# Two expert weight loads issued before the last four modulation blocks, and two gate diagonals built after the head norm, in a two-layer diffusion trunk

## What is computed

```python
for i in range(DEPTH):                       # DEPTH = 2
    sh1, sc1, g1, sh2, sc2, g2 = modulation(cvec, w_ada[i], b_ada[i])   # for c_ctx and for c
    h = rmsnorm(x, norm_g[i, 0]) * (1.0 + sc1) + sh1
    if i % 2 == 0:
        y, s = hgrn2_mixer(h, hgrn_w_in, lb, hgrn_onorm_g, hgrn_w_out, s0)
    else:
        y = diff_attn_out(diff_attention(q, k, v, lam), attn_subln_g, lam_init, attn_w_out)
    x = x + g1 * y
    h = rmsnorm(x, norm_g[i, 1]) * (1.0 + sc2) + sh2
    x = x + g2 * hier_moe(h, w_group, b_group, w_expert, b_expert, w_gate, w_up, w_down)
# the end of the HGRN2 mixer: a norm over each head, a SiLU gate, the output matrix
o = rmsnorm(o, onorm_g) * silu(g)
return o @ w_out
```

## Time and profile before

| | |
|---|---|
| time, median of 3 runs | 1291.94 us (1291.27 to 1293.31) |
| profiled execution: its own time | 1291.27 us |
| profiled execution: span | 1289.5 us |
| PE busy | 1127.8 us (87%) |
| DVE busy | 427.3 us (33%) |
| ACT busy | 228.2 us (18%) |
| POOL busy | 135.8 us (11%) |
| bytes moved | 316.78 MB, mean 246 GB/s |

### The profile page before, as it was taken

The page is one execution under the profiler, slowest core; times in us unless marked ns, Lnnn a source line. Parts: engine busy times, 40 slices in busy tenths (PEclk is TensorE's granted clock), DMA queues, the critical chain, the costliest instruction groups (busy, mean ns, idle before and its releaser), DMA issues.

```text
span 1289.5 us, 20237 instructions
## 1 busy us (share of the span) xinstructions
PE 1127.8 (87%) x8500; PEld 681.7 (53%) x8500; DVE 427.3 (33%) x1102; ACT 228.2 (18%) x527; POOL 135.8 (11%) x219
## 2 busy tenths in 40 slices
PE   4899999995999979998888499997779799988884
PEld 1566666664444465665665154443445656566651
DVE  1155555555512333000000754513853330000006
ACT  2201101110212222010001121104742221000110
POOL 0333333334000000000000300000000000000012
PEclk8899999997899979999999799998989799999997
DMA  9964444433557836999999952232001279999994
GB/s 342 290 203 131 132 132 132 132 132 132 180 201 267 352 142 263 409 428 427 426 426 426 396 211 89 78 118 98 1 1 52 80 277 419 427 426 427 426 425 169
DMA packets 97581, 316.78 MB, mean 246 GB/s; under 512 B 3792, under 2 KB 38912, under 8 KB 81120
## 3 DMA queue, kind: packets, MB, share of 16 engines
q1 hardware_dynamic: 90160, 298.05, 60.1%
q10 hardware_dynamic: 5248, 10.97, 2.2%
q0 software_dynamic: 2096, 6.67, 1.4%
HBM read 304.67 MB, written 11.01 MB: 245 GB/s over the span
## 4 chain that ended last, share of the span: by engine, by line
issue 71%; DVE 2%; DMA 2%; POOL 1%; PE 0%; POOLq 0%; DVEq 0%
DMA xn<-expert_rows,moe_row 2%; DVE xn L1520 1%; DVE moe_own L1518 0%; DVE xn L1523 0%; DVE moe_own L1530 0%; DVE hg_att L1563 0%; POOL x L1878 0%; POOL moe_own L1873 0%; DVE hg_tf L1580 0%; DVE hg_qaf L1600 0%; DVE hg_kf L1602 0%; DVE x L1535 0%; POOL hg_kb L1843 0%; POOL hg_qab L1841 0%; PE bank L702 0%
## 5 line engine op out<-in xcount | busy, mean ns | idle before, releaser
L566 PE MATMUL bank<-ring,moe_xe 128*64 128x256 f32 x2048 | 229.8, 380 | 29.5 <-DMA ring<-in_moe_w_up 16.9
L566 PEld LDWEIGHTS bank<-ring,moe_xe 128*64 128x64 f32 x2048 | 152.1, 137 | 111.3 <-DMA ring<-in_moe_w_up 21.4
L668 PE MATMUL bank<-uT,ring 128*128 128x384 f32 x384 | 137.3, 504 | 4.6 <-DMA ring<-in_hgrn_w_in 4.6
L581 PE MATMUL bank<-ring,moe_hT 128*64 128x512 f32 x512 | 118.3, 616 | 16.6 <-DMA ring<-in_moe_w_down 14.4
L855 PE MATMUL bank<-ring,uT 128*128 128x512 f32 x288 | 126.3, 593 | 1.3 <-issue 1.3
L1508 DVE TENSOR_TENSOR moe_hh<-moe_sg,bank 128x256 f32<-128x256 f32 x32 | 13.5, 422 | 324.1 <-ACT moe_sg L1032 324.1
L554 PE MATMUL bank<-moe_g,moe_h 128*128 128x128 f32 x768 | 96.7, 285 | 2.4 <-DVE moe_g L1405 2.4
L554 PEld LDWEIGHTS bank<-moe_g,moe_h 128*128 128x128 f32 x768 | 92.7, 200 | 7.9 <-issue 7.9
L668 PEld LDWEIGHTS bank<-uT,ring 128*128 128x128 f32 x384 | 70.8, 193 | 47.1 <-ACT uT L954 4.8
L1869 POOL TENSOR_TENSOR moe_flag<-con 128x1 f32<-128x1 f32 x2 | 0.4, 194 | 897.1 <-DMA expert_rows<-moe_oe 897.1
L855 PEld LDWEIGHTS bank<-ring,uT 128*128 128x128 f32 x288 | 53.6, 190 | 65.1 <-issue 65.1
(11 more groups left out here) (249 smaller groups left out, 1203.8 us busy)
## 6 DMA issues: line engine op xcount, KB each, us to landing
ring<-in_moe_w_gate SPq DMA_DIRECT2D x32, 2048.0 KB, 24.4
ring<-in_moe_w_up SPq DMA_DIRECT2D x32, 2048.0 KB, 26.3
ring<-in_moe_w_down SPq DMA_DIRECT2D x32, 2048.0 KB, 23.0
ring<-in_w_ada SPq DMA_DIRECT2D x24, 2048.0 KB, 10.3
ring<-in_hgrn_w_in SPq DMA_DIRECT2D x32, 512.0 KB, 6.6
ring<-in_attn_w_qkv SPq DMA_DIRECT2D x6, 2048.0 KB, 22.2
expert_rows<-moe_oe ACTq DMA_DIRECT2D x14, 512.0 KB, 10.3
ring<-in_hgrn_w_in SPq DMA_DIRECT2D x2, 2048.0 KB, 13.4
```

What stands on the lines that cost most here:

```text
L566: last = mm(bank[2 + e][64 * g:64 * g + 64, 256 * part:256 * part + 256], m["xe"][:, k, 64 * e:64 * e + 64], cols(slot)[:, k, 256 * g:256 ...
L581: last = mm(bank[5 + 2 * half][64 * e:64 * e + 64, :], m["hT"][:, e, j, 64 * g:64 * g + 64], down_rows(PART_SLOTS[n][4 + e])[:, g, j, 512 ...
L668: last = mm(to[:, 0:TOK], w[:, k, f, :], uT[:, k, :], start=(k == 0), stop=(k == KC - 1))
```

## The change

Two edits in one.

The first is in SP's part: the first two loads of expert weights of layer 0 (gate and up of expert 0, into slots 2 and 3) are issued behind block 7 of the next layer's modulation, no longer behind block 11. `experts(0)` leaves them out in its first pair.

The second is in VectorE's part: the diagonals for q = 0 and q = 1 are made behind the head norm, directly ahead of `gated(0)`.

```diff
@@ SP
                     for at, (slot, (name, e)) in enumerate(zip(PART_SLOTS[n], PARTS)):
-                        expert_weights(n, i, it, slot, name, e)
+                        if at >= 2 or n == 1 or not isinstance(it, int) or it > 0:
+                            expert_weights(n, i, it, slot, name, e)
...
-            for b in range(12):
+            for b in range(8):
+                ada(1, b % 2, b, 5 + b // 2)
+            for slot, (name, e) in zip(PART_SLOTS[0][0:2], PARTS[0:2]):
+                expert_weights(0, 0, 0, slot, name, e)
+            for b in range(8, 12):
                 ada(1, b % 2, b, 5 + b // 2)
             count = experts(0)
@@ VectorE
             dve.wait_ge(hg["o_out"], 8)
-            need(dve, 0, "mod_cols", 12)
-            gate_diagonal(0, HG["diag"], 2, 0, 0)
-            gate_diagonal(0, HG["diag"], 2, 0, 1)
             dve.wait_ge(late_in, LATE)
             head_norm(0, HG["s0"][:, 0:8, :].rearrange("p h d -> p (h d)"))
             head_norm_end(0, None)
...
+            need(dve, 0, "mod_cols", 12)
+            gate_diagonal(0, HG["diag"], 2, 0, 0)
+            gate_diagonal(0, HG["diag"], 2, 0, 1)
             gated(0)
             gate_diagonal(0, HG["diag"], 2, 0, 2)
             gated(1)
```

## The result

| | before | after |
|---|---|---|
| median of 4 runs | 1291.88 us (1291.27 to 1293.31) | 1307.84 us (1305.93 to 1312.56) |
| profiled execution: own time | 1291.27 us | 1305.98 us |
| profiled execution: span | 1289.5 us | 1304.1 us |

The changed kernel is slower: its time divided by that of before is 1.0128, 95% interval [1.0099, 1.0156]. I had said 1304.0 us, 1297.5 to 1307.0. The direction and each of the places were right; the median lies 3.8 us above the number and 0.8 us above the range.

What follows compares the result with a forecast made beforehand. The prediction took TensorE's own list to bound the stage of the change. Its terms, 4.7 + 2.4 + 4.2 + 2.3 - 0.5 = +13.1 us on 1291.27, gave 1304.4, stated as 1304 us, range 1297.5 to 1307.

Steps and rivals of the forecast that it cites:

- term 1: Ahead of the first gate product, TensorE waits for the first diagonal, now made behind the head norm: +4.7 us.
- term 2: Behind the wait for the first diagonal, TensorE's clock falls to 0.50: +2.4 us, bounds 0 and 2.6.
- term 3: In the modulation, block 8 lands late behind gate and up in SP's queue: +4.2 us, bounds 2.3 and 5.6.
- term 4: Behind the wait for block 8, TensorE's clock falls again: +2.3 us, bounds 0 and 2.6.
- term 5: Block 11 of the modulation, no longer queued beside gate and up, is not waited for: -0.5 us.
- head start: At the first expert matmul, gate and up landing some 32 us earlier wins nothing, as they were early already.
- What bounds the stage: From 333 to 440 us TensorE's own list sets the end; its waits are lost, others' earlier work wins nothing.
- The diagonals: On VectorE the move costs nothing, but TensorE waits for the first diagonal, 4.7 us; the second costs nothing.
- The clock: An idle TensorE drops to 1.2 GHz and works slowly after each new wait: 2.4 and 2.3 us lost.
- only the diagonals: Rival: block 8 comes in time or under a microsecond late, so only the diagonals cost; 1297.9 us, chance 0.18.
- the clock holds: Rival: TensorE waits for the first diagonal and block 8, but its clock does not fall; 1299.7 us, chance 0.06.
- the head start counts: Rival: the expert weight stream sets the end, so 4 MB sent earlier take 9.8 us off; 1288.6 us, chance 0.04.

Runs made afterwards that it cites:

- e3: The changed kernel, both edits, profiled and timed once more against the kernel before: ratio 1.0100, median 1309.09 us.
- e1: The kernel before with only the two diagonals (q = 0 and 1) moved behind the head norm, loads in their old order: ratio to before 1.0077.
- e2: The kernel before with only gate and up of expert 0 issued behind block 7, diagonals still ahead of the head norm: ratio to before 1.0060.
- e4: The kernel before, unchanged, profiled and timed again against itself: ratio 0.9998.
- run 23: Not one run but a count: the kernel before, unchanged, timed 23 times beside the follow-up kernels; median 1293.81 us, 1289.8 to 1298.3.

## Why the prediction was right or wrong

| step | predicted | profile after | other profiles |
|---|---|---|---|
| term 1, wait for the first diagonal | 4.7 | 4.50 | 4.50, 4.49 (e3, e1) |
| term 2, clock behind it | 2.4 | 1.7 | 2.6, 2.7 (e3, e1) |
| term 3, wait for block 8 | 4.2 (2.3 to 5.6) | 6.0 | 6.4, 5.25 (e3, e2) |
| term 4, clock behind it | 2.3 | 1.8 | 1.7, 2.4 (e3, e2) |
| term 5, block 11 | -0.5 | -0.6 | nothing to win against e4, where block 11 did not wait |
| head start | 0 | 0 | 0 |
| sum | +13.1 | +13.5 in the stage | +14.4 (e3) |

**What bounds the stage**: right. TensorE's list set the end; all it lost arrived at the first expert matmul and at the end of the span.

**The diagonals**: right, and shown by the kernel with only the second one moved. The wait is 0.2 us shorter than I worked out.

**The clock**: right, shown by filling the waits. The single numbers scatter by 1 us with how long TensorE, back at work, still ran at 0.50: about 3.8 us behind block 8 in the changed kernel (1.8 us lost), 5.4 us behind the diagonal in the kernel with the diagonals alone (2.7 us lost).

**Block 8, term 3, failed in size**: the mechanism was right (order of the queue; shown by one load instead of two, and by the other place), but 4.2 us were forecast and 6.0 measured. I had two numbers from the same rows: 5.6 us late by the order of landing, 4.1 by counting bytes, and I took the bytes. Three profiles say 5.25, 6.0 and 6.4. The landing order gives it well: block 8 lands 5.3 to 5.4 us behind up in all of them. The byte count, with undisturbed rates and one fixed cost of 3.1 us for the whole row of four, was short: from block 7's issue to block 8's landing it has 24.1 us, and 25.1, 25.9 and 26.3 us were measured. All of the error is in the three loads ahead of block 8. The count has up land 18.5 us after block 7's issue; the same trio in the rows of before needed 20.0, and these three profiles have 19.7, 20.5 and 20.9. The 5.6 us for block 8 itself were, if anything, too long. The even mixing of block 8 with up, my lower bound of 2.3 us, did not happen. Nor did what the Trainium skill allows ("DMA: Bandwidth & Descriptors", Queues, rings and completion order), that a later transfer completes ahead of an earlier one of the same queue: for the loads of this stage no profile here shows it.

**The sum**: that the stage came out 0.4 us beside it is luck in part. Term 3 was 1.8 us short, and terms 1, 2, 4 and 5 together 1.5 us too high.

**The step from the sum to the number failed too**, and it is what put the median above the range. I anchored on one profiled execution of the kernel before, 1291.27 us, the fastest of three, and rounded 1304.4 down to 1304 although I had just said that it lay below the median. The range had the bounds of the terms and nothing for the scatter. The kernel before, run 23 times more, has a median of 1293.81 us and spreads over 8.5 us, and an attention stage can differ by 6 us with the clock. From 1293.81 the same sum gives 1306.9. The forecast ratio, 1304.0 / 1291.94 = 1.0093, lies just under the first interval and within that of the repeat.

**The rivals**: "only the diagonals", "the clock holds" and "the head start counts" did not occur. No block beside 8 was late.

## What to carry to other kernels

Before a load is moved forward in an in-order queue, look at the load behind it: when is it issued, when wanted, how much slack has it, and how long does the queue stand idle before it. What is put ahead of it costs its transfer less that idle time: here 1.8 us for the first 2 MB and 4.4 for the second. Moving both to another queue, in the one place where it was tried, only made another block late. Before work is moved behind other work on an engine with time to spare, look for who waits for its first piece; it may be enough to leave that piece in place. And where the engine that bounds a stage must wait for some microseconds, count its clock as well: in this stage each wait of 4.5 to 6.4 us cost another 1.7 to 2.7, and matmuls without a use in waits that were there anyway won 0.9%.

## What the runs showed of the hardware that I had not expected

- Two loads of expert weights (2 MB, rows of 16 KB) on ScalarE's queue took 8.6 and 13.9 us beside a load of `w_ada` (2 MB in pieces of 2 KB) issued at the same time on SP's queue, which took 18.6 us. The two queues did not share evenly. From 393 to 411 us ScalarE's queue moved 4.19 MB in 288 packets, SP's 2.37 MB in 1174. The Trainium skill ("DMA: Bandwidth & Descriptors", Queues, rings and completion order) says that an engine goes round its queues by packets; that would favour the one with larger pieces, but no run here separates the size of the pieces from the queue.
- One kernel's time moves by microseconds from run to run with nothing changed. The largest piece that the profiles show is the attention stage, in which TensorE idles for over a microsecond in each round: 66.0 us at a mean clock of 0.94 or 71.8 us at 0.86.
- In the stage of the change the clock held behind a wait of 0.79 us and fell with every wait of about 4.5 us or more. In the attention the same short idle time went either way: TensorE idled for 1.56 us ahead of 903.82 in the kernel before and then ran at 1.00; it idled for 1.57 us ahead of 911.98 in the kernel with the loads alone and then ran at 0.50.
